# Two-block transformer kernel on one core: products of 512 columns, slots picked head by head, a reordered begin, and a rearranged end of the first attention stage

## The chip, the cores and the metric

The kernel runs on one core of a Trainium2 chip. The time is the device time of one execution in microseconds (us). Of the kernel before there are three runs: median 2908.13 us, from 2906.12 to 2909.43 us. One further execution was profiled, and took 2918.25 us; from its first to its last instruction it spans 2916.5 us, and all rows below come from it.

## The reference

A sequence of 256 tokens with 1024 channels (and a second, `mem`, of 256 tokens) passes through two transformer blocks of two layers each. Cut to what matters here:

```python
# first block, per layer
x = x + g_a * (attention(norm(x) @ w_in) @ w_out)
x = x + g_f * ((silu(h @ w_gate) * (h @ w_up)) @ w_down)     # D_FF = 2816
# second block, per layer
x = x + mixer(...)
x = x + cross_attention(norm(x), norm(mem))                  # xa_wq, xa_wkv, xa_wo
x = x + peer_ffn(norm(x))
# peer_ffn: 8 heads, 128 x 128 experts
scores = q @ sub_keys            # two halves per head
top_s, top_i = top_k(scores, 16)
cand = top_s[0][:, None] + top_s[1][None, :]      # 256 candidates
best_s, best_pos = top_k(cand, 16)
expert_idx = take(top_i[0] * 128 + top_i[1], best_pos)
a = h . u[expert_idx];  y = sum(softmax(best_s) * gelu(a) * v[expert_idx])
```

The kernel computes `a` for all 16384 experts and multiplies by a matrix of gates that is zero outside the picked ones. All large products are in float32 precision by three products of fp32r numbers: a number is split in a high part and a low remainder, and high x high, high x low and low x high are summed.

## The kernel before, in words

**Units.** All weights come as 438 units of 128 x 2048 floats (1 MB), in one order (`lists`). The sync engine (SP) loads a unit into one of three buffers `raw` (`fetch`, L2191). ScalarE (ACT) copies it, rounded, to `whi` (L891, `upto`), VectorE (DVE) subtracts and gets the remainder `wlo` (L1329, `through`), and TensorE (PE) multiplies. `whi` and `wlo` have two buffers each; `whi` of unit k+2 waits until PE has read the high part of unit k. Each engine's program calls `take()` once for each unit, and does its stage work between the calls in written order. There are 48 further loads of modulation weights, which DVE accumulates (`modulate`, L1342, L1345).

**Forms.** In an A unit (`a_unit`) the weight is the stationary operand and the activations move: for each of two groups n of output columns and each q of eight, one product with the high part `hth` (L401) and one with the low part `htl` (L403), each of 256 moving columns, into one half of one PSUM bank; then 16 products of `wlo` with `hth` (L411). That is 48 matmuls of 256 columns. B and C units (`b_unit`, L427 to L438; `c_unit`, L453 to L463) have 24 matmuls of 512 columns, with the activations stationary. The 196 A units that the change touches are: w_gate and w_up of both layers (44), xa_wq (8), peer_wq (16), and the expert matrix u (128). The other 16 keep their form. PE takes banks 4 to 7 in turn where none is named (`Banks.take`), and waits until ACT or DVE has read what the bank held (`clear`).

**The peer stage of a layer.** PE: 8 units pq, each followed by the score products of the head before (L825, banks 0 to 3); then 64 units of u (counted u = 0 to 63); then 64 C units of v. ACT applies GELU to each bank of u (L1277). DVE finds the 16 best by MAX8, FIND_INDEX8 and MATCH_REPLACE8 (`sixteen`, L1777 to L1787; `select_head`), in small steps that `some(us)` hands out between the units: steps of 2.2 nominal us for each pq unit and 2.7 for each u unit below 29. After all eight heads `select_slots` turns positions into expert numbers for one half of the tokens at a time: an IS_EQUAL of 2048 elements (`pick`, L1820), eight multiplications on GpSimd (POOL, L2165), a sum (`red`, L1826). At u = 29 PE transposes the result (L848), and from u = 30 to 57 DVE makes one-hot matrices (`one_hot`, L1897 to L1902), PE multiplies them (`gate`, L838), and DVE applies them (`weigh`, L1912). The other half of the gates is made beside the first 31 C units.

**The feed-forward stage.** For each i of 11: unit g, unit u, then the C unit `down(i - 1)`. ACT applies SiLU to g (L1101), DVE multiplies by u (L1646), ACT and DVE split the result.

**The begin.** The memory's normalized transpose, three units K, the transposes of x, the modulation sums (L375, after eight modulation loads), and the fourth K unit. Then `first_mixer(0)`: 12 B units for q, k, v, the heads' scores, weights and values (`step`), filled up with V units, then two transposes (`out_part`), a `gate_row` (L382), and four C units.

## Time and profile before

| | |
|---|---|
| median of 3 runs | 2908.13 us (2906.12 to 2909.43) |
| profiled execution, its own time | 2918.25 us |
| its span | 2916.5 us |
| TensorE busy | 2818.6 us (97%) |
| VectorE busy | 1971.7 us (68%) |
| ScalarE busy | 1336.6 us (46%) |
| GpSimd busy | 194.7 us (7%) |
| moved by DMA | 537.78 MB, mean 184 GB/s |

Matmuls are pipelined: a row's duration is longer than the distance from one start to the next. The rate of a series is read from the starts.

### The profile page before, as it was taken

To read this page: it belongs to the slowest core of one execution; us is meant where nothing else is said; L and a number is where in the kernel's file an instruction comes from. 1 tells how busy PE (TensorE), PEld (TensorE's weight loads), DVE (VectorE), ACT (ScalarE), POOL (GpSimd) and SP (SyncE) were. 2 spreads that over 40 slices of the span, in tenths; PEclk is the share of its full clock that TensorE was granted. 3 is DMA by queue.
4 is the path that set the end of the run, shared out by engine and by line. 5 is a ranking of instruction groups with operands and counts; after the bars stand their busy time and mean duration, and the time that the engine had idled before them with its cause. 6 is when DMAs were issued, how large, how long until landed. Compare 5 with 4: busy or idle time off the path is not lost.

```text
span 2916.5 us, 45834 instructions
## 1 busy us (share of the span) xinstructions
PE 2818.6 (97%) x19604; PEld 2547.9 (87%) x19604; DVE 1971.7 (68%) x2790; ACT 1336.6 (46%) x1454; POOL 194.7 (7%) x168
## 2 busy tenths in 40 slices
PE   7889999999999899999999999998999999999998
PEld 6768998789988789999988888897899999988887
DVE  6767766664443558877769965535589777699755
ACT  3454435554457444443434444484444534344443
POOL 0200002010003000220000000030000500000000
PEclk9989999999999999999999999999999999999999
DMA  7848864645543345554445555533455544455554
GB/s 294 292 147 303 306 214 148 213 173 188 185 182 130 130 157 176 174 188 160 173 154 193 174 188 193 217 130 118 156 174 177 185 163 170 160 188 174 188 191 148
DMA packets 75658, 537.78 MB, mean 184 GB/s; under 512 B 8512, under 2 KB 8896, under 8 KB 12096
## 3 DMA queue, kind: packets, MB, share of 16 engines
q1 hardware_dynamic: 75456, 534.86, 52.0%
q8 instruction: 155, 2.54, 0.3%
q14 instruction: 47, 0.39, 0.0%
HBM read 527.48 MB, written 7.34 MB: 183 GB/s over the span
## 4 chain that ended last, share of the span: by engine, by line
PE 63%; issue 22%; DVE 6%; POOL 3%; ACT 3%; DMA 2%; SPq 0%; DVEq 0%; POOLq 0%; ACTq 0%
PE bank L401 10%; PE bank L411 10%; PE bank L403 10%; PE bank L453 7%; PE bank L455 6%; PE bank L463 6%; POOL big L2165 2%; PE bank L427 2%; PE bank L429 2%; PE bank L438 2%; DVE wlo L1329 2%; PE bank L491 2%; DMA raw<-in_wkv 1%; PE bank L838 1%; ACT whi L891 1%
## 5 line engine op out<-in xcount | busy, mean ns | idle before, releaser
L891 ACT ACTIVATE whi<-raw 128x2048 fp32r<-128x2048 f32 x438 | 839.3, 1917 | 1073.2 <-PE bank L403 544.8
L1329 DVE TENSOR_TENSOR wlo<-raw,whi 128x2048 fp32r<-128x2048 f32 x438 | 1007.8, 2301 | 424.4 <-ACT whi L891 424.0
L401 PE MATMUL bank<-hth,whi 128*128 128x256 f32 x3392 | 835.1, 286 | 3.4 <-DVE htl L1399 1.9
L403 PE MATMUL bank<-htl,whi 128*128 128x256 f32 x3392 | 824.7, 283 | 0.0
L401 PEld LDWEIGHTS bank<-hth,whi 128*128 128x128 f32 x3392 | 649.4, 191 | 8.7 <-DVE htl L1394 3.3
L403 PEld LDWEIGHTS bank<-htl,whi 128*128 128x128 f32 x3392 | 650.0, 192 | 1.2 <-issue 0.5
L453 PE MATMUL bank<-whi,hth 128*128 128x512 f32 x1152 | 459.1, 399 | 14.4 <-DVE htl L1394 10.0
L455 PE MATMUL bank<-whi,htl 128*128 128x512 f32 x1152 | 451.9, 392 | 0.0
L411 PE MATMUL bank<-hth,wlo 128*128 128x256 f32 x3392 | 441.9, 283 | 1.0 <-DVE wlo L1329 1.0
L411 PEld LDWEIGHTS bank<-hth,wlo 128*128 128x128 f32 x3392 | 422.2, 192 | 1.4 <-DVE wlo L1329 1.4
L463 PE MATMUL bank<-wlo,hth 128*128 128x512 f32 x1152 | 287.4, 389 | 0.0
L453 PEld LDWEIGHTS bank<-whi,hth 128*128 128x128 f32 x1152 | 218.2, 189 | 61.6 <-issue 15.8
L455 PEld LDWEIGHTS bank<-whi,htl 128*128 128x128 f32 x1152 | 218.1, 189 | 44.2 <-issue 0.2
L463 PEld LDWEIGHTS bank<-wlo,hth 128*128 128x128 f32 x1152 | 216.2, 188 | 44.9
L1399 DVE TENSOR_TENSOR htl<-big,hth 128x512 fp32r<-128x512 f32 x144 | 99.3, 690 | 178.7 <-ACT hth L917 178.7
L1912 DVE SCALAR_TENSOR_TENSOR big<-bank,big 128x512 f32<-128x512 f32 x128 | 127.9, 1006 | 25.5 <-PE bank L838 19.6
L427 PE MATMUL bank<-whi,hth 128*128 128x512 f32 x288 | 118.4, 411 | 7.4 <-ACT whi L891 7.4
L429 PE MATMUL bank<-whi,htl 128*128 128x512 f32 x288 | 115.3, 400 | 0.0
L2091 POOL TENSOR_TENSOR small<-small 128x2 f32<-128x2 f32 x12 | 8.4, 702 | 1432.9 <-DVE small L1375 1432.9
L917 ACT ACTIVATE hth<-big 128x512 fp32r<-128x512 f32 x144 | 88.3, 614 | 31.4 <-DVE big L1411 27.8
L2165 POOL TENSOR_TENSOR big<-big 128x256 f32<-128x256 f32 x64 | 77.9, 1256 | 353.7 <-DVE big L1820 353.7
L491 PE MATMUL bank<-small,big 128*128 128x128 f32 x384 | 63.3, 341 | 36.4 <-DVE small L1385 34.0
(255 smaller groups left out, 2978.8 us busy)
## 6 DMA issues: line engine op xcount, KB each, us to landing
raw<-in_pu SPq DMA_DIRECT2D x128, 1024.0 KB, 4.8
raw<-in_pv SPq DMA_DIRECT2D x128, 1024.0 KB, 4.8
raw<-in_win SPq DMA_DIRECT2D x52, 1024.0 KB, 4.8
big<-in_wmod SPq DMA_DIRECT2D x24, 1024.0 KB, 7.2
raw<-in_wmod SPq DMA_DIRECT2D x24, 1024.0 KB, 5.2
raw<-in_wgate SPq DMA_DIRECT2D x22, 1024.0 KB, 4.9
raw<-in_wup SPq DMA_DIRECT2D x22, 1024.0 KB, 5.0
raw<-in_wdown SPq DMA_DIRECT2D x22, 1024.0 KB, 4.9
```

The lines of the kernel that those rows point to most:

```text
L401: e.matmul(o[n], h[:, q, c[n]], H[:, q * 256:(q + 1) * 256], start=n == 0 and q == 0, stop=False, skip_group_check=True)
L403: m = e.matmul(o[n], h[:, q, c[n]], L[:, q * 256:(q + 1) * 256], start=False, stop=False, skip_group_check=True)
L411: m = e.matmul(o[n], w[:, q, c[n]], H[:, q * 256:(q + 1) * 256], start=False, stop=q == 7, skip_group_check=True)
L427: e.matmul(psum(keys[t])[:, :], H[:, o:o + 128], h[:, q, :], start=half == 0 and q == 0, stop=False, skip_group_check=True)
L429: m = e.matmul(psum(keys[t])[:, :], L[:, o:o + 128], h[:, q, :], start=False, stop=False, skip_group_check=True)
L453: e.matmul(bank[i][:, :], H[:, x:x + 128], h[:, q, c], start=opens and q == 0, stop=False, skip_group_check=True)
L455: m = e.matmul(bank[i][:, :], L[:, x:x + 128], h[:, q, c], start=False, stop=False, skip_group_check=True)
L463: m = e.matmul(bank[i][:, :], H[:, x:x + 128], w[:, q, i % 2 * 512:(i % 2 + 1) * 512], start=False, stop=closes and q == 1, skip_group_che ...
L891: e.activation(whi(j), slot[u][0], ACT.Copy).then_inc(*hi.mark(j))
L1329: e.tensor_tensor(wlo(j), slot[u][0], whi(j).bitcast(F32), ALU.subtract).then_inc(*lo.mark(j))
L1912: e.scalar_tensor_tensor(v, product, 1.0 / 1024, v, ALU.mult, ALU.mult).then_inc(*took_v.mark(key))
L2165: e.tensor_tensor(eh, eh, tf, ALU.mult).then_inc(*p_mul.mark((l, "pick", t, w)))
```

## The change

1. `a_unit` becomes `wide_unit` for the 196 units: `hth` and `htl` are interleaved in one tile (`Halves`: for each of 8 chunks 256 columns high, then 256 low), so that one matmul of 512 columns does the work of L401 and L403. It fills a whole bank: the left half gets high x high and (by the 16 matmuls of 256 columns) low x high, the right half high x low. The unit takes two banks, aligned (`Banks.pair`: 4 and 5, or 6 and 7). ACT copies the left halves out (`apart`), DVE adds the right halves (`joined`), and GELU or SiLU is then applied in SBUF, one unit later.
2. The slots are picked head by head (`select_slots(l, h)`, `slots_summed(l, h)`) instead of after all heads; shares and softmax once for all. `some` gets 3.0 for each pq unit from the third, 2.4 for each u below 30. The slots are transposed at u = 32 instead of 29 (`GATES`), and gates are made from u = 32 to 57, two in every fourth unit instead of every eighth.
3. Begin: another order of modulation and K units; x is loaded earlier, lambda and rope gains later; x is transposed before the third K unit, and K units 2 and 3 go to banks 1 and 2.
4. End of the first attention stage of layer 0: the last weights and values use other banks (0, 1, 4 and 6, 7), the first two `out_part` go to step 13, `gate_row(0, 0)` goes behind the second of the four C units, and its modulation loads come earlier.

```diff
+class Halves:
+    def __init__(self, x):
+        v = x.rearrange("p (c h n) -> p c h n", h=2, n=256)
+        self.both, self.hi, self.lo = x, v[:, :, 0], v[:, :, 1]
...
+    def pair(self, key):
+        self.turn += self.turn % 2
+        b = 4 + self.turn % 4
+        self.turn += 2
...
+        def wide_unit(key, M, ready, between=None):
+            for n in range(2):
+                evicted(held[n])
+                for q in range(8):
+                    if n == 0 and q % 2 == 0:
+                        ready(q // 2)
+                    m = e.matmul(bank[b + n], h[:, q, c[n]], M.both[:, q * 512:(q + 1) * 512], start=q == 0, stop=False,
...
+            on.wait_ge(*lo.at(k))
+            for n in range(2):
+                for q in range(8):
+                    m = e.matmul(bank[b + n][:, 0:256], w[:, q, c[n]], M.hi[:, q], start=False, stop=q == 7,
...
-    units += [m0[0], m0[1], k0[0], m0[2], k0[1], m0[3], m0[4], k0[2], *m0[5:], k0[3]]
+    units += [m0[0], m0[1], k0[0], m0[2], m0[3], k0[1], m0[4], m0[5], k0[2], m0[6], m0[7], k0[3]]
...
-            if l == 0:
-                gate_row(0, 0)
             project(("o1", l), ("mix1", l), OO)
...
                 if i == 1:
-                    out_part(name, o, 2)
-                    out_part(name, o, 3)
+                    if stage == ("mix1", 0):
+                        gate_row(0, 0, (4, 5))
+                    for q in (2, 3):
...
+        def apart(dst, key, k):
+            on.wait_ge(*unit.at(k))
+            e.copy(pair(dst), parts(key)[0]).then_inc(*took_a.mark(key))
...
+        def joined(dst, key):
+            on.wait_ge(*took_a.at(key))
+            e.tensor_tensor(pair(dst), parts(key)[1], pair(dst), ALU.add).then_inc(*took_v.mark(key))
...
 # ScalarE, expert units
             for u in range(64):
-                if u in (21, 25):
-                    exponent(u // 25)
+                if u == GATES - 1:
+                    exponent()
                 k = take()
                 upto(k + 2)
-                on.wait_ge(*unit.at(k))
+                if u:
+                    gelu(u - 1)
                 region(on, l, u)
-                e.activation(ag(u * 512, 512), psum(key)[:, :], ACT.Gelu).then_inc(*took_a.mark(key))
+                apart(ag(u * 512, 512), ("a", l, u), k)
+            gelu(63)
...
 # VectorE, expert units
                 take()
+                if u:
+                    activated(u - 1)
+                if u == GATES - 2:
+                    some(1e9)
+                    exponents(l)
+                if u == GATES - 1:
+                    shares(l)
+                if u == GATES:
+                    slots_turned(l, 0)
+                    slots_turned(l, 1)
+                if GATES <= u < 58:
                     gate_step(l, 0, *plan.step(pace(u)))
-                if u < 29:
-                    some(2.7)
+                if u < GATES - 2:
+                    some(2.4)
```

`select_slots(l, h)` does, for both token halves in one instruction each: a cast of 32 indices, shift, mask and two casts of 16, and two IS_EQUAL of 512 elements; POOL multiplies four times 256 elements for each head; `slots_summed` is two sums over 512 elements, done after the next head's search.

## Rows read from the trace of the kernel before

**Rows 1.** The page's first part: busy time, share of the span, instructions
```profile
PE 2818.6 (97%) x19604; PEld 2547.9 (87%) x19604; DVE 1971.7 (68%) x2790; ACT 1336.6 (46%) x1454; POOL 194.7 (7%) x168
```
**Rows 2.** TensorE's waits, expert units of layer 0, 1063 to 1500 us
```profile
PE bank L411 <- DVE wlo L1329: 0.5, 1, 0.5
```
**Rows 3.** Chain of waits, two A units in a row: start us, us, what
```profile
1145.28 1.92 PE bank L411 x16
...
1151.04 1.92 PE bank L411 x16
```
**Rows 4.** Timeline of TensorE, two C units in a row: start us, us, instruction
```profile
1696.90 0.39 PE L453 MATMUL bank<-whi,hth 128*128 128x512 f32 x1
...
1700.53 1.98 PE L463 MATMUL bank<-wlo,hth 128*128 128x512 f32 x8
1702.34 0.39 PE L453 MATMUL bank<-whi,hth 128*128 128x512 f32 x1
```
**Rows 5.** Stretches: start:end us, length, PE, PEld, DVE, ACT, POOL, clock, DMA share, GB/s
```profile
283.17:419.00 135.83, 135.83 (x962) 128.17 (x962) 92.84 (x53) 55.51 (x40) 0.00 (x0) 1.00 0.76 277
1112.00:1170.00 58.00, 58.00 (x486) 58.00 (x486) 54.83 (x193) 27.80 (x23) 0.00 (x0) 1.00 0.55 189
1279.00:1440.00 161.00, 161.00 (x1644) 160.01 (x1643) 119.79 (x168) 63.80 (x52) 0.00 (x0) 1.00 0.50 171
1145.49:1197.31 51.82, 51.82 (x434) 51.82 (x433) 47.45 (x161) 22.19 (x19) 0.00 (x0) 1.00 0.53 183
```
**Rows 6.** Groups of VectorE and ScalarE: shapes, count | busy us, mean ns | idle before
```profile
L1424 DVE TENSOR_TENSOR big<-bank,big 128x512 f32<-128x512 f32 x24 | 16.1, 688 | 10.6 <-PE bank L463 10.6
L1912 DVE SCALAR_TENSOR_TENSOR big<-bank,big 128x512 f32<-128x512 f32 x128 | 127.9, 1006 | 25.5 <-PE bank L838 19.6 <-ACT big L1277 5.9
L1399 DVE TENSOR_TENSOR htl<-big,hth 128x512 fp32r<-128x512 f32 x144 | 99.3, 690 | 178.7 <-ACT hth L917 178.7
L1277 ACT ACTIVATE big<-bank 128x512 f32<-128x512 f32 x128 | 76.4, 597 | 0.6 <-PE bank L411 0.5
```
**Rows 7.** Timeline of VectorE, one unit with gates: start us, us, instruction
```profile
1317.98 2.29 DVE L1329 TENSOR_TENSOR wlo<-raw,whi 128x2048 fp32r<-128x2048 f32 x1 [0.20 <-ACT whi L891]
1320.19 0.42 DVE L1897 TENSOR_TENSOR oh<-iotah,tj 128x512 f16<-128x512 f16 x1
...
1321.80 1.28 DVE L1912 SCALAR_TENSOR_TENSOR big<-bank,big 128x512 f32<-128x512 f32 x2
```
**Rows 8.** Timeline of VectorE while POOL multiplies, 1222 to 1246 us
```profile
1228.35 2.83 DVE L1329 TENSOR_TENSOR wlo<-raw,whi 128x2048 fp32r<-128x2048 f32 x1
1233.21 2.29 DVE L1826 TENSOR_REDUCE big<-big 128x128 f32<-128x2048 f32 x1 [2.03 <-POOL big L2165]
```
**Rows 9.** Groups of GpSimd: the multiplications of the slots
```profile
L2165 POOL TENSOR_TENSOR big<-big 128x256 f32<-128x256 f32 x64 | 77.9, 1256 | 353.7 <-DVE big L1820 353.7
```
**Rows 10.** Timeline of TensorE, first matmul after the last expert unit u
```profile
1501.86 0.76 PE L453 MATMUL bank<-whi,hth 128*128 128x512 f32 x1 [1.98 <-issue]
```
**Rows 11.** The same place as a stretch, columns as in rows 5: eight matmuls
```profile
1501.86:1505.34 3.48, 3.48 (x9) 2.77 (x9) 3.48 (x9) 0.00 (x0) 0.00 (x0) 0.51 0.00 0
```
**Rows 12.** TensorE's waits, begin of the kernel, 0 to 130 us
```profile
PE bank L491 <- DVE small L1385: 11.8, 2, 10.5
PE bank L427 <- ACT whi L891: 6.7, 3, 4.0
PE bank L491 <- ACT big L956: 2.3, 1, 2.3
PE bank L401 <- DVE big L1411: 2.1, 1, 2.1
```
**Rows 13.** TensorE's waits, the last heads of layer 0, 190 to 212 us
```profile
PE bank L574 <- ACT big L1047: 2.6, 1, 2.6
PE bank L562 <- DVE big L1578: 2.2, 2, 1.4
PE bank L544 <- ACT big L950: 1.0, 1, 1.0
```
**Rows 14.** The begin as a stretch, columns as in rows 5
```profile
60.00:115.00 55.00, 49.44 (x218) 40.11 (x216) 42.50 (x58) 23.93 (x26) 14.91 (x3) 0.94 0.76 269
```

More of the change, by code:

```diff
@@ L25 @@
 NRAW = 3
+GATES = 32
 NSP = 2
@@ L91, in take @@
         self.held[b] = key
+        self.where[key] = b
+        return b, before
+    def pair(self, key):
+        self.turn += self.turn % 2
+        b = 4 + self.turn % 4
+        self.turn += 2
+        before = [self.held.get(b), self.held.get(b + 1)]
+        self.held[b] = self.held[b + 1] = key
         self.where[key] = b
@@ L188, in program @@
     IOTAH = at("iotah", 204800 + 4 * 1888, 128, F16)
-    bank = [ctx.enter_context(nc.psum_tensor(f"bank{i}", [P, 512], F32)) for i in range(8)]
+    PS = ctx.enter_context(nc.psum_tensor("banks", [P, 4096], F32))
+    bank = [PS[:, i * 512:(i + 1) * 512] for i in range(8)]
     banks = Banks()
@@ L194, in psum, with parts, pair @@
         return bank[banks.where.get(key, 0)]
+    def parts(key):
+        b = banks.where.get(key, 0)
+        v = PS[:, b * 512:(b + 2) * 512].rearrange("p (n h c) -> p n h c", n=2, h=2)
+        return v[:, :, 0], v[:, :, 1]
+    def pair(x):
+        return x.rearrange("p (c n) -> p c n", n=256)
     def ag(o, n):
@@ L353, in tensor, with evicted @@
         used = [0]
-        def clear(key, b=None):
-            b, held = banks.take(key, b)
+        def evicted(held):
             if took_a.has(held):
@@ L360, in clear @@
                 on.wait_ge(*took_v.at(held))
+        def clear(key, b=None):
+            b, held = banks.take(key, b)
+            evicted(held)
             return b
@@ L389, in take, with a_unit @@
             return k
-        def a_unit(key, H, L, ready, between=None, b=None):
+        def wide_unit(key, M, ready, between=None):
+            k = take()
+            b, held = banks.pair(key)
+            h, w = whi(k).rearrange("p (k n) -> p k n", k=8), wlo(k).rearrange("p (k n) -> p k n", k=8)
+            c = [slice(n * 128, (n + 1) * 128) for n in range(2)]
+            for n in range(2):
[4 more added lines that the diff above has]
+                    m = e.matmul(bank[b + n], h[:, q, c[n]], M.both[:, q * 512:(q + 1) * 512], start=q == 0, stop=False,
+                                 skip_group_check=True)
+                if n == 0 and between is not None:
+                    between()
+            m.then_inc(*hi_read.mark(k))
+            on.wait_ge(*lo.at(k))
+            for n in range(2):
+                for q in range(8):
+                    m = e.matmul(bank[b + n][:, 0:256], w[:, q, c[n]], M.hi[:, q], start=False, stop=q == 7,
+                                 skip_group_check=True)
+            m.then_inc(*unit.mark(k))
+            return k
+        def a_unit(key, M, ready, between=None, b=None):
             k = take()
@@ L531, in first_mixer @@
                     turn_query(nb - 3)
-                b_unit(keys, HTH, HTL, 1, lambda q: normed(on, name, q))
+                b_unit(keys, HT, 1, lambda q: normed(on, name, q))
             turn_query(3)
             def scores(nq, hs):
-                of = [bank[clear(("s", l, nq, h))] for h in hs]
+                last = l == 0 and nq and hs[0] == 6
+                of = [bank[clear(("s", l, nq, h), 4 + h % 2 if last else None)] for h in hs]
                 on.wait_ge(*took_a.at(("qt", l, nq, 1)))
@@ L583, in step @@
                     scores(2, (2 * (i - 8), 2 * (i - 8) + 1))
+                if l == 0 and i == 13:
+                    for q in range(2):
+                        out_part(("o1", l), OO, q, 5 - 5 * q)
                 if 2 <= i < 14:
@@ L1094, in feed_forward @@
             for i in range(11):
+                gate, hd = (ag(PR + 1024 * x + (i % 2) * 512, 512) for x in range(2))
                 k = take()
                 upto(k + 2)
-                on.wait_ge(*unit.at(k))
                 if i >= 2:
@@ L1198, in query @@
                 key = ("xq", l, h)
-                on.wait_ge(*unit.at(k))
                 since()
-                e.copy(ag(QTX + h * 512, 512), psum(key)[:, :]).then_inc(*took_a.mark(key))
+                apart(ag(QTX + h * 512, 512), key, k)
                 last_h[0] = k
@@ L1258, in peer @@
                     k = take()
[L1259 to L1260 removed]
                     since()
[L1262 removed]
+                    apart(ag(QT + i * 512, 512), ("pq", l, i), k)
                 if i:
@@ L1633, in feed_forward @@
             for i in range(11):
+                gate, hd = (ag(PR + 1024 * x + (i % 2) * 512, 512) for x in range(2))
                 k = take()
@@ L1865, in selection, with slots_summed @@
+        def slots_summed(l, h):
+            for w in range(2):
+                on.wait_ge(*p_mul.at((l, "pick", h, w)))
+                dst = ag(II, 768).rearrange("p (t w k) -> p t w k", t=2, w=3)[:, :, w, h * 16:(h + 1) * 16]
+                e.tensor_reduce(dst, picked(h, w), X, ALU.add).then_inc(*top.mark((l, "red", h, w)))
+                yield 0.65
         def selection(l):
```

387 lines of the change are left out of this document (198 added, 189 removed).

## The prediction

> **What bounds the kernel now.** I read the page's busy times first: TensorE is busy in 97% of the span, VectorE in 68% [rows 1]. Then TensorE's waits by stage. From 1063 to 1500 us, the pq and u units of a layer, it waits 0.5 us in all [rows 2]; nothing is to be had there but fewer or cheaper matmuls. The begin and the last heads of layer 0 are where it does wait [rows 12, 13]. Third, the rate. Sixteen matmuls of 256 columns take 1.92 us, 120 ns each, and an A unit repeats every 5.76 us, which is 48 of them [rows 3]. A C unit repeats every 5.44 us, 24 matmuls of 512 columns at 226.7 ns, and its first 16 take 3.63 us [rows 4]. At 2.4 GHz the columns alone are 106.7 and 213.3 ns, so about 13.3 ns per matmul come on top at either length. That is what fewer, longer matmuls can save. Last, VectorE by stage: 54.8 of 58 us busy at u = 0 to 9, 119.8 of 161 in the stage with gates, 92.8 of 135.8 in the feed-forward [rows 5]. The engine that gets new work is nearly full exactly where most of the changed units are.
>
> **The change, part by part.**
>
> *Wide matmuls.* Per unit 32 matmuls of 256 columns (3.84 us) become 16 of 512 (3.63 us at the rate of rows 4); the 16 low ones stay. A unit goes from 5.76 to 5.55 us, 0.214 less; times 196 units, -42 us. All lies on the path, since TensorE sets it. Bounds: no saving, if a 512 costs two 256 (0), and 16 x (240 - 213.3) = 0.43 us per unit (-84), if the extra vanished. I take the C unit's rate: the same length, a new stationary block for each matmul as here.
>
> The trace shows 120 ns where columns take 106.7 [rows 3]. The Trainium skill (TensorE: Matmul & The Clock Gate, "Back-to-back issue gap") gives a warm gap of columns / 2.4 + 2.5 ns; by it a pair is worth 2.5 ns and this part an estimated 8 us, not 42. The trace does not agree with the 2.5.
>
> *New eviction.* ACT now copies the left halves (0.60 us, the nearest row is GELU out of a bank) and applies GELU or SiLU later from SBUF (0.6 again) [rows 6]. Its load is 27.8 of 58 us [rows 5], so +0.6 per unit is covered by TensorE's 5.55. DVE adds the right halves. Nearest row: one bank and one SBUF input of 512, 688 ns; upper bound the strided 1006 ns [rows 6]. I take 0.66 to 0.69, the plain add. In the feed-forward, DVE has 92.8 of 135.8 us, eight triples; two adds per triple make 104 of 132: covered, as is ACT. The `down` unit needs its input only two units later. Cross attention: the pairs make q2 and q3 wait for the add of the unit before, about 1.4 us after it, behind score products of about that length: nothing.
>
> *DVE while slots are picked, u = 0 to 29.* From 1145.49 to 1197.31 us lie nine units and three heads; DVE is busy 47.45 us [rows 5]. Less nine `wlo` at 2.21 (distance of starts, rows 7) that is 9.2 us per head. New per head are two IS_EQUAL and two sums over 512 elements at about 0.66 (as L1399, rows 6) and five tiny ones, 0.65 together: 3.3. So 12.5 us per head for a nominal 11.7; a handful of 2.4 nominal costs 2.56. DVE per unit: 2.21 + 0.67 + 2.56 = 5.44, beside TensorE's 5.55. POOL's 64 multiplications of 1.26 us [rows 9] no longer come in a block behind the search but 5 us in each head. While POOL runs, `wlo` takes 2.83 instead of 2.29 us, while a sum with one input keeps its 2.29 [rows 8]. One `wlo` and one IS_EQUAL per head meet it: +0.7 per head, +0.14 per unit: 5.58. A tie. Handfuls are uneven, and a late add holds up TensorE's next pair: I take 2 us per layer, +4. Bounds: 0 (5.44 is below 5.55) and, with an add of 1.0 us, 5.9, that is 0.35 x 30 x 2 = +21.
>
> That only two-input operations stretch fits the Trainium skill (SBUF — State Buffer, "Who interferes with whom"): such a DVE instruction and a GpSimd one that reads SBUF contend, and the loser fully blocks. By full blocking each such meeting could cost a whole POOL instruction; that is in the third rival.
>
> *Gates in 26 instead of 28 units.* DVE per unit: 2.21 + 0.67 + one-hot 1.61 (1320.19 to 1321.80) + 0.65 for applying [rows 7], 5.1; with two gates 7.4. TensorE needs 6.1 to 6.65. Sum over 26 units: about 147 against 157 to 162 us. Covered, 0.
>
> *The transposes at u = 32.* They take two banks, which are unit 30's; unit 32's aligned pair is then unit 31's, just finished. It waits for `joined(31)`, which on DVE stands behind `wlo` of the unit after next: 2.2 + 0.7 = 2.9 us, less 0.6 for the transposes. A stall of 2.4 us in each layer. After the idle 1.98 us at 1501.86 [rows 10] the granted clock was 0.51, the lower of its two levels (1.2 GHz), and eight 512s took 3.48 instead of 1.81 us [rows 11]: +1.7. So +4.1 per layer, +8. Bounds: 2.4 and 4.1 per layer.
>
> *From u to v.* That 1.98 us is GELU, split, remainder. Now it is copy 0.6, add 0.7, GELU 0.6, split 0.6, remainder 0.7: 3.3, +1.3 per layer, +2.6. The slow clock there is already paid. *The last score of pq* waits for an add more, 0.6 per layer, +1.2.
>
> *Begin.* The K units, 5.8 us each, now partly stand between the transposes and the modulation sums. The waits for the diagonal behind a modulation load, the 2.3 and 2.1 us [rows 12] can shrink, and the first B unit can start some 4 us earlier. But then come waits for `whi`, 6.7 us, behind DMA at 269 GB/s and 76% [rows 12, 14], which take back part. Lambda and rope gains are issued behind the first freed raw buffer, at about 25 us, and are needed at 47 and 67 us. I take -3; bounds 0 and -12 (half of the 22.9 us in rows 12). *End of the stage:* the waits of the last heads, 5.8 us [rows 13], get 1 us of transposes to fill them, and the gate row fills another gap: -2; bounds 0 and -4.
>
> **Sum:** -42 + 4 + 8 + 2.6 + 1.2 - 3 - 2 = -31 us. The profiled execution, 2918.25 us of its own, would take 2887; its time is 10.1 us above the median shown, and the difference goes against the median: **2908.1 - 31 = 2877 us**. Of this, TensorE's matmuls are -42 and the new waits +16.
>
> **The rivals.**
>
> (1) *DVE is a little over TensorE while slots are picked.* Add at 1.0 us, 5.9 per unit, +21 instead of +4: 2894 us. For: DVE had 54.8 of 58 us. Against: the plain add from a bank is 0.69. Chance 0.18.
>
> (2) *The begin gives more.* If the reordering gives back some 20 us of the idle in rows 12 and 13, 2862 us. For: 28.7 us stand there. Against: DMA at 269 GB/s. Chance 0.10.
>
> (3) *Slower: DVE becomes the bound of the expert units.* Without DVE's term the sum is -35, so it decides from a loss of 35 us in the 60 units below u = 30: 5.55 + 0.58 = 6.1 us of DVE per unit. Adds at 1.0 (+0.33) and three DVE operations per head blocked by a whole POOL instruction of 1.26 us (3.8 / 4.9 units = +0.77) give 5.44 + 1.1 = 6.5: +57, so 2930 us. For: two-input operations do stretch [rows 8]. Against: by 0.54, not by 1.26. Chance 0.05.
>
> (4) *The change doesn't save what it says:* if only a fifth of the 13.3 ns per pair were saved in this form (weights stationary, activations moving), the first part gives 8 us and the whole is +3: 2911 us. This is the time to which the page's 2.5 ns leads. Against: C units show the full amount [rows 4]. Chance 0.03.
>
> **How the numbers follow.** Forecast 0.64, with a range of its own of 2864 to 2890. About 0.2% (6 us) can be told from no change. Forecast, (1) and (2) are faster by more: 0.92. (4) is within: 0.03. (3) is slower: 0.05. Range 2858 to 2898: it takes in (1) and (2) at their values and leaves out (3), (4) and the far ends of (1) and (2).
>
> **What would show it.** Right: A units of u repeat every 5.55 us, with 16 matmuls of 512 in 3.63; `joined` takes 0.69; before unit 32 TensorE idles about 2.4 us in each layer, with a clock below 1.00 behind it, and before v = 0 about 3.3 us; DVE is over 95% busy for u below 30. Wrong: a period of 5.7 or more with waits for DVE (rival 1 or 3); `wlo` often at 2.8 us or more; pairs of starts 240 ns apart (rival 4); TensorE waiting in the feed-forward, which I cost at nothing; or a begin shorter by more than 10 us (rival 2).

## The result, and the profile after

The changed kernel takes 2902.1 us (median of 16 runs, 2898.9 to 2906.4). The kernel before, with as many runs in turn on the same chips, takes 2916.4 us (2906.1 to 2926.4). The ratio is 0.9953, 95% interval 0.9942 to 0.9965: about 14 us faster. The forecast was 2877 us, 31 us below the median shown then. Some 8 us of the miss in the absolute time come from that base: 2908.1 us was the median of three runs, and the wider sample lies at 2916.4, close to the profiled execution's 2918.25. The other 17 us are the change's own: it gained half of what the sum said.

The page of the kernel after, first its busy times, then the groups that are new (line, engine, operation, names and shapes, count | busy us, mean ns | idle before):

```profile
PE 2791.4 (96%) x16468; PEld 2382.6 (82%) x16468; DVE 2090.9 (72%) x3086; ACT 1408.0 (49%) x1620; POOL 192.0 (7%) x168
...
L428 PE MATMUL banks<-ht,whi 128*128 128x512 f32 x3136 | 771.5, 395 | 7.4 <-DVE big L1470 5.4
...
L976 ACT COPY big<-banks 128x512 f32<-128x512 f32 x196 | 112.2, 572 | 72.7 <-PE banks L436 72.2
L1470 DVE TENSOR_TENSOR big<-banks,big 128x512 f32<-128x512 f32 x196 | 133.8, 683 | 9.7 <-ACT big L976 9.0
```

Against [rows 1], 3136 matmuls are gone (196 units times 16). The new add, `joined` (L1470), takes 683 ns: the plain add of [rows 6], as taken. The new copy takes 572 ns.

The timeline of TensorE, one wide expert unit and the start of the next (start us, us, instruction), answers to [rows 3]:

```profile
1130.48 3.82 PE L428 MATMUL banks<-ht,whi 128*128 128x512 f32 x16
1134.13 2.08 PE L436 MATMUL banks<-ht,wlo 128*128 128x256 f32 x16
1136.04 1.32 PE L428 MATMUL banks<-ht,whi 128*128 128x512 f32 x5
```

Sixteen wide products take 3.65 us from start to start, 228 ns each, and the unit repeats every 5.56 us where it took 5.76. That is close to the forecast for a unit that holds nothing else (3.63 and 5.55 us). TensorE's waits of the expert stage of layer 0, 1063 to 1500 us, tell more. [Rows 2] had 0.5 us of waits for the low parts, and the 1.98 us of [rows 10] behind the last unit:

```profile
PE banks L503 <- DVE ht L1465: 3.9, 1, 3.9
...
PE banks L880 <- DVE big L1470: 3.0, 1, 3.0
PE banks L428 <- DVE big L1470: 2.7, 1, 2.7
```

Three single waits, all behind the new chain of copy and add. Stretches of the kernel after (columns as in [rows 5]): the feed-forward; early expert units in two pieces, slots being picked; just behind the wait at unit 32; units with gates.

```profile
283.17:419.00 135.83, 135.83 (x728) 117.73 (x727) 102.59 (x70) 65.70 (x59) 0.00 (x0) 1.00 0.77 279
...
1106.30:1161.90 55.60, 55.60 (x321) 49.18 (x320) 55.15 (x141) 30.06 (x30) 12.60 (x10) 1.00 0.55 189
1161.90:1278.80 116.90, 116.90 (x673) 103.30 (x673) 109.38 (x281) 62.75 (x65) 22.49 (x19) 1.00 0.55 190
1284.30:1288.00 3.70, 3.69 (x9) 2.93 (x10) 3.67 (x11) 0.00 (x0) 0.00 (x0) 0.54 0.87 283
1304.50:1480.00 175.50, 175.50 (x1376) 151.86 (x1375) 145.66 (x199) 82.50 (x87) 0.00 (x0) 1.00 0.50 169
```

In the first ten units in which slots are picked, VectorE is busy 55.15 of 55.60 us, 99%, in the next 21 units 109.38 of 116.90, 94%, and TensorE does not wait once. The tie that the forecast saw is there in the first ten, and it costs nothing.

Everything below is measured with one ruler, worked out from TensorE's timeline of one execution of each kernel: the distance from the first product of the first query unit of an expert stage to the first product of its first down unit, in parts. Here and in all runs, us, layer 0 / layer 1 where they differ:

| kernel | queries to u=0 | u=0 to 31 | 31 to 32 | 32 to 63 | 63 to v=0 | sum |
|---|---|---|---|---|---|---|
| before | 53.89 | 180.07 | 6.31 | 195.19 | 7.89 | 443.4 |
| after | 56.60 / 56.42 | 172.66 / 174.16 | 9.10 | 192.35 | 9.58 | 440.3 / 441.6 |
| E1 slots' banks | 56.56 / 56.42 | 172.66 / 174.15 | 6.14 | 191.66 | 9.58 | 436.6 / 438.0 |
| E2 add first | 53.71 / 53.75 | 175.42 / 175.44 | 9.10 | 190.76 | 9.58 | 438.6 |
| E3 narrow ends | 53.08 / 53.50 | 174.45 / 174.41 | 9.10 | 192.3 | 8.39 | 437.3 / 437.8 |
| E4 = E1 and E3 | 53.06 | 174.44 | 6.14 | 191.66 | 8.39 | 433.7 |
| E5 two of 256 | 57.03 / 57.15 | 180.13 / 179.67 | 9.29 | 195.56 / 197.04 | 9.76 | 451.8 / 452.9 |
| E6 slots part alone | 53.89 | 178.64 | 6.33 | 195.57 | 7.90 | 442.3 |
| E7 more picking | 56.46 / 56.58 | 181.27 / 181.30 | 9.10 | 192.34 | 9.58 | 448.8 / 448.9 |
| E8 four pairs | 53.06 / 53.48 | 172.67 | 6.18 | 191.68 | 8.40 | 432.0 / 432.4 |
| E10 E8, GELU first | 53.44 | 172.67 | 6.18 | 191.69 | 7.94 | 431.9 |

One thing disturbs this ruler. After a wait of 2.6 to 3 us TensorE's granted clock is sometimes 1.00 and sometimes near the lower of its two levels, and the lower level makes the unit behind the wait 1.0 to 1.6 us longer. This is in unit 0 (second part) or unit 32 (fourth part), and it is named below where a comparison hangs on it.

An expert stage gave only 3.1 and 1.7 us up to the down units, 2.4 on average. In the profiled execution (span 2916.5 before, 2900.3 after) the rest of the 16.2 us comes from the two feed-forwards, 4.3 and 3.5, and from the begin and first attention stage, 4.6 (237.3 to 232.8 us); the other stages together take about 1 us more than before.

### The profile page after: what moved, and what is told of

Its sections match the earlier page's. It is cut to its first block and busy times, and to the rows that moved or that the text cites. A ratio compares the mean times of both kernels' runs of the same rounds, so it can differ in the third digit from the quotient of the medians.

```text
span 2900.3 us, 40006 instructions
## 1 busy us (share of the span) xinstructions
PE 2791.4 (96%) x16468; PEld 2382.6 (82%) x16468; DVE 2090.9 (72%) x3086; ACT 1408.0 (49%) x1620; POOL 192.0 (7%) x168
## 5 line engine op out<-in xcount | busy, mean ns | idle before, releaser
L428 PE MATMUL banks<-ht,whi 128*128 128x512 f32 x3136 | 771.5, 395 | 7.4 <-DVE big L1470 5.4
L428 PEld LDWEIGHTS banks<-ht,whi 128*128 128x128 f32 x3136 | 576.5, 189 | 123.3 <-issue 6.9
L503 PE MATMUL banks<-whi,ht 128*128 128x512 f32 x1152 | 459.6, 399 | 18.2 <-DVE ht L1460 10.0
L505 PE MATMUL banks<-whi,ht 128*128 128x512 f32 x1152 | 452.7, 393 | 0.0
L436 PEld LDWEIGHTS banks<-ht,wlo 128*128 128x128 f32 x3136 | 401.9, 191 | 15.8
L436 PE MATMUL banks<-ht,wlo 128*128 128x256 f32 x3136 | 406.6, 283 | 0.0
L513 PE MATMUL banks<-wlo,ht 128*128 128x512 f32 x1152 | 287.4, 389 | 0.0
L503 PEld LDWEIGHTS banks<-whi,ht 128*128 128x128 f32 x1152 | 218.6, 190 | 65.3 <-issue 19.3
L505 PEld LDWEIGHTS banks<-whi,ht 128*128 128x128 f32 x1152 | 218.7, 190 | 44.3
L513 PEld LDWEIGHTS banks<-wlo,ht 128*128 128x128 f32 x1152 | 216.2, 188 | 44.9
L1470 DVE TENSOR_TENSOR big<-banks,big 128x512 f32<-128x512 f32 x196 | 133.8, 683 | 9.7 <-ACT big L976 9.0
L2002 DVE SCALAR_TENSOR_TENSOR big<-banks,big 128x512 f32<-128x512 f32 x128 | 127.3, 1005 | 18.4 <-PE banks L893 18.4
L477 PE MATMUL banks<-whi,ht 128*128 128x512 f32 x288 | 116.9, 406 | 8.2 <-ACT whi L946 8.2
L479 PE MATMUL banks<-whi,ht 128*128 128x512 f32 x288 | 114.0, 396 | 0.0
```

The source lines that it names most:

```text
L428: m = e.matmul(bank[b + n], h[:, q, c[n]], M.both[:, q * 512:(q + 1) * 512], start=q == 0, stop=False, skip_group_check=True)
L436: m = e.matmul(bank[b + n][:, 0:256], w[:, q, c[n]], M.hi[:, q], start=False, stop=q == 7, skip_group_check=True)
L477: e.matmul(psum(keys[t])[:, :], M.hi[:, half * 4 + q, o], h[:, q, :], start=half == 0 and q == 0, stop=False, skip_group_check=True)
L479: m = e.matmul(psum(keys[t])[:, :], M.lo[:, half * 4 + q, o], h[:, q, :], start=False, stop=False, skip_group_check=True)
L503: e.matmul(bank[i][:, :], M.hi[:, o + q, x], h[:, q, c], start=opens and q == 0, stop=False, skip_group_check=True)
L505: m = e.matmul(bank[i][:, :], M.lo[:, o + q, x], h[:, q, c], start=False, stop=False, skip_group_check=True)
```

## The experiments

Each run is compared, as the change was, with runs of the kernel before on the same chip; a difference from the kernel after is that of the two ratios times 2917 us, and is uncertain by some 5 us. The table above is the sharper measure.

**E1. The slots' transposes in other banks.**

```diff
-                        b = clear(("top", l, t))
+                        b = clear(("top", l, t), 2 + t)
```

> The changed kernel, but the transposes of the picked slots at unit 32 go to banks 2 and 3 (used by the scores long before) instead of banks 4 and 5, so that unit 32 takes the pair of banks that unit 30 used and not the one that unit 31 has just filled. Theory A (time is lost where PE waits for the sum of a pair of banks): the 2.7 us wait of PE for the sum of unit 31 goes, and with it the stretch of slow clock behind it; unit 32 takes 6.2 to 6.5 us from the start of the transposes where it took 10.8, so about -4.5 us per layer, -9 us in all, ratio to the kernel before 0.9953 to about 0.992. Rival B (VectorE has no room here and is late anyway, so that the wait moves to the next units): the units 33 to 36 take up the time, and the total changes by less than 2 us.

Measured: 2895.8 us, ratio 0.9919 (0.9905 to 0.9933), 10 us less than after; 3.7 us per layer in the table, 7.3 in all. The place before, in the kernel after, and then in E1 (timeline of TensorE):

```profile
1280.79 0.85 PE L903 MATMUL banks<-small,big 128*128 128x128 f32 x6
1284.31 5.50 PE L428 MATMUL banks<-ht,whi 128*128 128x512 f32 x16 [2.68 <-DVE big L1470]
1289.65 2.07 PE L436 MATMUL banks<-ht,wlo 128*128 128x256 f32 x16
```

```profile
1281.50 0.82 PE L903 MATMUL banks<-small,big 128*128 128x128 f32 x6
1282.07 3.91 PE L428 MATMUL banks<-ht,whi 128*128 128x512 f32 x16
1285.82 2.08 PE L436 MATMUL banks<-ht,wlo 128*128 128x256 f32 x16
...
1289.57 0.64 PE L893 MATMUL banks<-oh 128*128 128x64 f16 x16
1290.94 0.64 PE L893 MATMUL banks<-oh 128*128 128x64 f16 x16 [0.73 <-DVE oh L1992]
```

The wait and the slow products behind it (granted clock 0.54 in 1284.30 to 1288.00) are gone; from the start of the transposes to unit 33 it is 6.23 us instead of 10.77. Of these 4.5 us 0.9 come back in unit 33 (7.53 us in E1, 6.63 after), at a gate whose one-hots VectorE has not ready: another wait was hidden behind this one. Theory A holds, at four fifths of its size.

**E2. VectorE makes the last query sum first.**

```diff
-                    some(3.0 if i > 1 else 0.0)
+                    some({1: 0.0, 7: 0.0, 8: 6.0}.get(i, 3.0))
```

> The changed kernel, but VectorE picks nothing between the sums of query units 6 and 7 of an expert stage, and twice as much right behind the sum of unit 7. No operation is added or removed. Theory A: the last score of the queries waits for a sum that VectorE could have made 3 us sooner; PE's wait of 3.0 us falls to about 0.5 us, the interval of that score from 10.7 and 12.4 us to about 8, so -3 to -4 us per layer, about -7 us in all, ratio about 0.993. Rival B (the cost is VectorE's load, not its order): the double handful makes the weights' low parts of the first units late, PE waits there, and the total changes by less than 2 us.

Measured: 2901.3 us, ratio 0.9938 (0.9924 to 0.9951), 4 us less than after. The cause is seen in the timeline of VectorE in the kernel after:

```profile
1096.75 0.68 DVE L1470 TENSOR_TENSOR big<-banks,big 128x512 f32<-128x512 f32 x1
1097.35 0.75 DVE L1878 TENSOR_TENSOR big<-big 128x256 f32<-128x256 f32 x2
...
1100.25 0.74 DVE L1865 MAX8 big<-big 128x8 f32<-128x256 f32 x2
1100.91 0.67 DVE L1470 TENSOR_TENSOR big<-banks,big 128x512 f32<-128x512 f32 x1
```

Between the sums of query units 6 and 7 stands a whole handful of picking, 3.6 us, while TensorE stands still for 2.99 us before the last score at 1101.64. In E2 (timeline of TensorE) that wait is 0.41 us, and a new one of 2.56 us stands before unit 2:

```profile
1102.09 1.16 PE L880 MATMUL banks<-big 128*128 128x128 f32 x8 [0.41 <-DVE big L1470]
...
1116.94 3.42 PE L428 MATMUL banks<-ht,whi 128*128 128x512 f32 x14 [2.56 <-DVE big L1470]
```

So both theories name something real. The order on VectorE made the wait; but the work moved behind the sum made VectorE late, and unit 2, which takes unit 0's pair of banks, paid for it. The table shows 2.9 and 2.7 us won up to u=0 and, in layer 0, 2.8 lost behind it. (In layer 1 the kernel after had lost 1.5 us there, in a stretch of slow clock behind the wait; that went, and the net loss is 1.3.) Unit 32 met no slow clock in this run, though TensorE's wait before it was as long as ever, 2.67 us. That is worth 1.6 us per layer in the fourth part and is not the edit's doing by any path that I can name. Without it the edit gains 1.5 us in both layers together, 1.4 of them in layer 1 by the slow clock that went, and that is less than the 2 us that theory B allowed: in the total it is B that holds.

**E3. Query unit 7 and unit 63 narrow again.** ScalarE takes the whole result out of one bank, and VectorE adds nothing there.

```diff
-                    wide_unit(("pq", l, i), HT, ready)
+                    (wide_unit if i < 7 else a_unit)(("pq", l, i), HT, ready)
...
-                wide_unit(("a", l, u), HT, ready, between)
+                (wide_unit if u < 63 else a_unit)(("a", l, u), HT, ready, between)
...
-                apart(ag(u * 512, 512), ("a", l, u), k)
-            gelu(63)
+                if u < 63:
+                    apart(ag(u * 512, 512), ("a", l, u), k)
+            on.wait_ge(*unit.at(k))
+            e.activation(ag(63 * 512, 512), psum(("a", l, 63))[:, :], ACT.Gelu).then_inc(*took_a.mark(("a", l, 63)))
...
```

> The changed kernel, but the two units of an expert stage whose result PE needs at once (query unit 7 and unit 63) are again made with 32 products of 256 columns into one bank, copied (or passed through GELU) by ScalarE alone, with no sum on VectorE. Theory A (the wait belongs to the chain copy, sum, GELU behind a wide unit): each of the four units costs 0.2 to 0.45 us more on PE, the last score falls from 10.7 and 12.4 us to about 7.8, and the gap between unit 63 and the first down unit from 3.85 to about 2.0 us (11.0 to 9.4 us with the products around it); about -5 us per layer, -10 us in all, ratio about 0.992. Rival B (VectorE's load or the slow clock at the change of stage makes these waits, whatever the form of the last unit): under 2 us.

Measured: 2889.2 us, ratio 0.9895 (0.9878 to 0.9911). The table gives 3.0 and 3.9 us per layer, 6.9 in all; the ratio says 17, with some 6 us of uncertainty, and I go by the table, though its execution was the longest of E3's four (2900.7 us; the others took 2886.8 to 2890.5). Why the whole time gained more than the expert stages is open. The last score no longer waits (queries to u=0: 53.1 to 53.5 us, below the kernel before). Waits of TensorE in E3, 1040 to 1500 us:

```profile
PE banks L428 <- DVE big L1476: 4.2, 2, 2.7
...
PE banks L503 <- DVE ht L1471: 2.5, 1, 2.5
```

The 4.2 us are unit 32's 2.7 and 1.5 us at unit 2: VectorE is still behind there, with the handful that now follows query unit 7. The gap behind unit 63 fell by 1.2 us, less than the 1.7 that the change had added.

**E4. E1 and E3 together.**

> Narrow query unit 7 and unit 63 together with the slots' transposes in banks 2 and 3. Theory A: the places lie apart on the path, so the two savings add up, -9 and -10 us to about -19 us, 2883 us, ratio about 0.989. Rival B (one VectorE schedule behind all of them): less than the larger one of the two alone plus 2 us.

Measured: 2890.3 us, ratio 0.9895 (0.988 to 0.9911). In the table 433.7 us per layer, 6.6 and 7.9 below the kernel after; E1 gave 3.7 and E3 3.0 and 3.9, so the sum would be 6.7 and 7.5. They add up, as theory A has it; in the whole time, 17 us by the ratios, E4 is not told apart from E3.

**E5. The wide product taken apart.** All units, sums and orders as in the kernel after, but two products of 256 columns for each of 512.

```diff
-                    m = e.matmul(bank[b + n], h[:, q, c[n]], M.both[:, q * 512:(q + 1) * 512], start=q == 0, stop=False,
-                                 skip_group_check=True)
+                    e.matmul(bank[b + n][:, 0:256], h[:, q, c[n]], M.hi[:, q], start=q == 0, stop=False,
+                             skip_group_check=True)
+                    m = e.matmul(bank[b + n][:, 256:512], h[:, q, c[n]], M.lo[:, q], start=False, stop=False,
+                                 skip_group_check=True)
```

> The changed kernel with all its two-bank units, sums and schedule, but each product of 512 columns is made as two of 256 again (the tile's high part into the first half of the bank, its low part into the second). This prices the wide product alone. Theory A (the unit's period is set by PE): the high part of a unit goes from 3.65 to about 3.84 us, the period from 5.565 to about 5.76, 196 units, +38 us, ratio about 1.008; the waits for the sums get shorter by what PE is later, so a little less, +30 to +38. Rival B (the units run at VectorE's pace, so PE's gain was already eaten): under +15 us.

Measured: 2935.2 us, ratio 1.0059 (1.0044 to 1.0074), so the wide form is worth 31 us; theory A holds, at the low end of its 30 to 38. Stage by stage it is 11.5 and 11.3 us for the two expert stages, 4.3 and 3.7 us for the two feed-forwards (200.1 against 195.8, 204.3 against 200.6 us), 30.8 in these four. A unit with nothing else in it gains 0.195 us, close to the 0.214 of the forecast. One with gates gains three quarters of it, 0.15 us: with one gate it takes 6.31 us in E5 and 6.16 in the kernel after, with two 6.77 and 6.63. The fourth part of the table says this in layer 1 alone, where it is 197.04 against 192.35, 0.15 per unit. In layer 0 it is 195.56 against 192.35, but there unit 32 met full clock in E5 (5.83 us) and the lower level in the kernel after (7.25 us). Unit 0 of layer 0 was the other way round (7.33 us in E5, 5.66 after), so that the sum of the layer is right by luck. Unit 32 of E5, its first 3.7 us in layer 0 and in layer 1 (columns as in [rows 5]):

```profile
1302.36:1306.06 3.70, 3.69 (x31) 3.70 (x32) 3.67 (x11) 0.00 (x0) 0.00 (x0) 1.00 0.83 283
2347.95:2351.65 3.70, 3.70 (x21) 3.70 (x22) 3.67 (x11) 0.00 (x0) 0.00 (x0) 0.65 0.79 288
```

The timelines of TensorE show where a unit with one gate loses part of the gain. First E5, then the kernel after:

```profile
1314.97 0.28 PE L428 MATMUL banks<-ht,whi 128*128 128x256 f32 x1
...
1316.89 0.64 PE L895 MATMUL banks<-oh 128*128 128x64 f16 x16
...
1319.36 2.08 PE L438 MATMUL banks<-ht,wlo 128*128 128x256 f32 x16
```

```profile
1304.35 2.00 PE L428 MATMUL banks<-ht,whi 128*128 128x512 f32 x8
1306.19 0.64 PE L893 MATMUL banks<-oh 128*128 128x64 f16 x16
1306.67 2.09 PE L428 MATMUL banks<-ht,whi 128*128 128x512 f32 x8
1308.60 2.07 PE L436 MATMUL banks<-ht,wlo 128*128 128x256 f32 x16
```

Eight wide products take 1.84 us ahead of the gate, where E5's sixteen take 1.92, and 1.93 behind it; in E5 gate and second half together take 2.47 us (1316.89 to 1319.36), here 2.41. The first half gains 0.08 and the second 0.06 us: the products right behind a gate take 0.09 us more than those ahead of it, and a quarter of the unit's gain is lost there. Of the two rules weighed in the forecast the trace's own 13.3 ns per product held (16 pairs give 0.195 us, 12 ns a pair). By the Trainium skill (TensorE: Matmul & The Clock Gate, "Back-to-back issue gap") a pair is worth an estimated 2.5 ns, 8 us in all, and these runs do not agree with it.

**E6. The slots part alone, on the kernel before.** The slots picked head by head, multiplied on GpSimd between, turned at unit 32, denser gates; products of 256 and no sums, and handfuls of 2.2 and 2.7 nominal us as before.

```diff
+GATES = 32
...
-                if u == 29:
+                if u == GATES:
...
-            for t in range(2):
-                yield from select_slots(l, t)
+                if h:
+                    yield from slots_summed(l, h - 1)
+                yield from select_slots(l, h)
...
```

> The kernel before with the slots part of the change alone: each head's slots picked right behind the head on VectorE and multiplied on GpSimd, the turned slots at unit 32 in place of 29, the first half's gates from unit 32. Products stay 256 columns wide into one bank, with no sums. Theory A (this part lies beside PE): no wait of PE for a sum exists here, so the ratio is 0.998 to 1.002. Rival B (the small loss per unit that gates show in the changed kernel comes from the denser gates of this part): +2 to +4 us, ratio 1.001 to 1.0015, with gated units about 0.05 us longer than before.

Measured: 2915.2 us, ratio 0.9988 (0.9976 to 0.9999): most likely 3.5 us faster, within theory A's bounds ("beside PE"). The table says why there is anything: units 0 to 31 take 1.43 us less, the transposes that stood at unit 29 and a wait for a low part in unit 26 (6.51 us, here 5.76), and units 32 to 63 take 0.38 more, because all the gates now stand there. In sum it is 1.0 us per layer. A unit with one gate takes 6.31 us here as in the kernel before, so rival B, a longer gated unit, is out. My forecast had no term for the stop at unit 29 that goes.

**E7. More picking beside each unit.** `some(2.4)` becomes `some(3.0)`; the same operations, sooner.

> The changed kernel with VectorE picking 3.0 us worth of the planner's costs beside each early expert unit in place of 2.4, so it is finished some five units sooner; no operation is added. VectorE is busy 55.15 of 55.60 us there already. Theory A (PE has no slack left to give VectorE: a unit's period is the larger of the two engines' work, one unit of lag is covered by the two pairs of banks): the period rises from 5.565 to about 5.9 to 6.1 us for some 22 units and PE waits for sums and low parts in each, +6 to +11 us per layer, ratio about 1.0 to 1.004. Rival B (VectorE catches up within the lag the banks allow): under +3 us in all.

Measured: 2919.2 us, ratio 1.0006 (0.9996 to 1.0016): 15.5 us more than after, all of it in units 0 to 31 (8.6 and 7.1 us per layer). A stretch (columns as before), and then the timeline of TensorE in E7 at its first wait:

```profile
1106.30:1161.90 55.60, 54.38 (x315) 47.95 (x314) 55.60 (x171) 30.17 (x30) 12.80 (x11) 1.00 0.53 178
```

```profile
1145.63 2.07 PE L436 MATMUL banks<-ht,wlo 128*128 128x256 f32 x16
1148.91 1.39 PE L428 MATMUL banks<-ht,whi 128*128 128x512 f32 x5 [1.22 <-DVE big L1470]
```

For eight units VectorE falls behind and nothing is seen. Then, from unit 8 on, TensorE waits for the sum of the unit two before it, 4.7 us in six waits of layer 0; 1.5 us of layer 0's 8.6 are slow clock at unit 0, as layer 1 of the kernel after has it, and the rest are tenths in the units around the waits. Theory A holds. VectorE at 99% costs nothing, and 0.6 nominal us more per unit cost 7.1 us in either layer, slow clock apart: the kernel after stands at this edge. The rivals (1) and (3) of the forecast name a real mechanism, which the measured 0.68 us of the add keeps out.

**E8. Four pairs of banks.** E3, and units 0 to 31 in turn in four pairs instead of two, the slots' transposes in banks 0 and 1.

```diff
-                wide_unit(("a", l, u), HT, ready, between)
+                if u < 32:
+                    wide_unit(("a", l, u), HT, ready, between, (4, 6, 0, 2)[u % 4])
...
-                        b = clear(("top", l, t))
+                        b = clear(("top", l, t), t)
...
```

> The kernel with narrow query unit 7 and unit 63, and units 0 to 31 in four pairs of banks in turn in place of two (the slots' transposes in banks 0 and 1), so that a unit waits for the sum of the unit four before it. Theory A (what PE waits for at unit 2 and unit 32 is the pair of banks, and VectorE's lag beyond one unit is otherwise harmless): both waits go; per layer the stretch from the first turn of the stage's input to the first down unit falls from 446.9 us (changed kernel) to about 437.5 us, that is 1.5 us below the narrow-ends kernel with the transposes moved (439.0), about 2880 us in all, ratio 0.989 to 0.987. Rival B (VectorE's lag would then hit the weights' low parts instead): PE waits for the low parts, and no gain beyond 439.0 us.

Measured: 2882.4 us, ratio 0.9879 (0.986 to 0.9898). Units 0 to 31 take 172.67 us, exactly 31 periods of 5.57; the wait at unit 2 that E3 and E4 had is gone. Waits of TensorE, 1045 to 1500 us, all there is:

```profile
PE banks L504 <- DVE ht L1477: 2.5, 1, 2.5
PE banks L894 <- DVE oh L2004: 0.8, 1, 0.8
```

Theory A: what TensorE waited for was the pair of banks. (The expectation's "stretch" counts from the turn of the stage's input: 437.4 us were expected, 437.4 and 438.9 measured, against 446.7 and 447.1 in the kernel after; the table's 432.0 and 432.4 leave out the turn, which itself differs by 1.1 us from layer to layer.)

**E9. The begin in the old order.** The order of the first weights and modulation blocks, of the tokens' turn and of the first transfers as before, and the K units' banks in turn as before; the rest as after.

```diff
-    units += [m0[0], m0[1], k0[0], m0[2], m0[3], k0[1], m0[4], m0[5], k0[2], m0[6], m0[7], k0[3]]
+    units += [m0[0], m0[1], k0[0], m0[2], k0[1], m0[3], m0[4], k0[2], *m0[5:], k0[3]]
...
```

> The changed kernel with the begin of the program in the order of the kernel before: the first memory-key weights and the modulation blocks in the old order, the tokens' turn behind the third key unit, the old order of the first transfers. The end of the first attention stage stays as changed. Theory A (the begin is worth what its rows showed, the third query unit starting at 72.7 in place of 77.0 us): +4 to +6 us, ratio 0.9953 to 0.997, with the third query unit at about 77 us again. Rival B (the first 240 us differ between executions of one kernel by as much, and the next wait for weights eats the gain): within 1.5 us, ratio below 0.996, although the third query unit starts later.

Measured: 2907.6 us, ratio 0.9969 (0.9957 to 0.998), 4.6 us more than after; and the expert stages as in the kernel after to 0.05 us. The third query unit in E9, and then in the kernel after (timeline of TensorE):

```profile
75.86 0.56 PE L477 MATMUL banks<-whi,ht 128*128 128x512 f32 x1 [3.16 <-ACT whi L945]
```

```profile
72.66 0.79 PE L477 MATMUL banks<-whi,ht 128*128 128x512 f32 x1 [6.16 <-ACT whi L946]
```

The new begin brings the query units forward by 6 to 7 us and then waits 3 us longer for weights, as the forecast said; 3.2 us are left here. By the ratios 4.6 us are left at the end, with an uncertainty of 5 us, so that the whole time alone would not exclude a value near nothing. At the modulation sums that end the first attention stage the two profiled executions are 7 us apart (239.7 and 232.7 us), which is within what executions of one begin differ by (last section). The 3.2 us and the ratio speak for theory A; the size is known to a few us only.

**E10. GELU of unit 62 first.** In E8, beside unit 63, ScalarE makes the GELU of unit 62 ahead of the next high part.

```diff
+                if u == 63:
+                    gelu(62)
                 upto(k + 2)
-                if u:
+                if 0 < u < 63:
                     gelu(u - 1)
```

> The four-pairs kernel, and beside unit 63 ScalarE makes the GELU of unit 62 ahead of the next weights' high part in place of behind it, so that it is done before unit 63 ends. Theory A (the 0.5 us by which the gap behind unit 63 is still longer than in the kernel before is that GELU): the stretch from unit 63's start to the first down unit falls from 8.40 to about 7.9 us, -1 us in all, ratio 0.987 to 0.988. Rival B (the high part of the next weights becomes what is late): 8.4 us or more, no gain.

Measured: 2883.2 us, ratio 0.9885 (0.9871 to 0.99). The wait before the first down unit is 2.0 us where E8 had 2.5, and 63 to v=0 is 7.94, as in the kernel before: theory A in the part, and nothing that the whole time could show. How the chain stood in the kernel after (timeline, ScalarE, VectorE and TensorE behind unit 63):

```profile
1482.38 0.61 ACT L1335 ACTIVATE big<-big 128x512 f32<-128x512 f32 x1
1482.90 0.57 ACT L976 COPY big<-banks 128x512 f32<-128x512 f32 x1
1483.50 0.69 DVE L1470 TENSOR_TENSOR big<-banks,big 128x512 f32<-128x512 f32 x1 [3.67 <-ACT big L976]
1484.22 0.63 ACT L1335 ACTIVATE big<-big 128x512 f32<-128x512 f32 x1 [0.76 <-DVE big L1470]
1484.76 1.13 ACT L972 ACTIVATE ht<-big 128x512 fp32r<-128x512 f32 x2
1485.41 0.69 DVE L1465 TENSOR_TENSOR ht<-big,ht 128x512 fp32r<-128x512 f32 x1 [1.21 <-ACT ht L972]
...
1486.24 0.77 PE L503 MATMUL banks<-whi,ht 128*128 128x512 f32 x1 [3.85 <-DVE ht L1465]
```

The first of these is the GELU of unit 62, which stood in the way of unit 63's copy. E8 and E10 are the fastest versions, 34 to 35 us below the kernel before by their ratios, where the change as made is 14 below.

## Why the prediction was wrong

The sum beside what was measured, both layers together, us. All are rows of one execution of each kernel; for the first, E5's ratio gives the same.

| step | forecast | measured | from |
|---|---|---|---|
| wide matmuls | -42 | -31 | E5 |
| VectorE while slots are picked | +4 | 0 | no wait for u = 1 to 31 |
| stall at unit 32 | +8 | +9.1 | 2 x (2.96 + 1.59), units 31 and 32 of after and E1 |
| last score of the queries | +1.2 | +7.9 | 3.1 and 3.3, and 1.5 of slow clock |
| from u to v | +2.6 | +3.7 | 2 x (1.69 + the 0.19 that the wide unit 63 saves) |
| begin and end of first stage | -5 | -4.6 | 237.3 to 232.8, uncertain by some us; E9 for the begin |
| slots part: stop at unit 29 gone, gates moved | 0 | -2.0 | 2 x 1.0; E6 |
| all other stages | 0 | +1 | spans |
| sum | -31 | -15.9 | span: -16.2 |

The sum closes to 0.3 us. Two terms made the miss, with 11 and 7 us; VectorE's term, 4 us too high, took some of it back.

**The term of the wide matmuls (-42) was too large.** The step was "0.214 less; times 196 units". The rate was nearly right for a unit that holds nothing else: 0.195 us, and the 44 feed-forward units, the 64 early expert units and the 12 last ones have it or come close. But 52 expert units, u=32 to 57, have small products in their middle, and 16 belong to the queries, with the scores' products between. E5 shows 0.15 us for the first kind; for the second, the seven intervals from query unit 0 to 7 take 46.31 and 45.92 us in E5 and 45.87 and 45.58 in the kernel after, 0.05 to 0.06 per unit. By these rows, as an estimate, the queries make 2.6 of the 11 us, the units with gates 3.5, and the rate itself (0.195 for 0.214 in the other 120) 2.3; the rest lies in the eight units of cross attention (21.83 us in E5 and 21.50 after for three intervals of layer 0) and in what one execution of each can't settle. I had looked at two C units in a row for the rate and never at a product that follows one of another shape, although the trace before had them in every one of those units.

**The last score (+1.2) was too small by 6.7 us.** "Waits for an add more, 0.6 per layer" priced the operation, and not the queue in front of it. The change adds a wait, and the rule that I followed at unit 32 (what stands ahead of the add on VectorE?) was not applied here: a handful of picking of 3.6 us. That the wait also drew a stretch of slow clock behind it, in layer 1 only (5.41 us for the next sixteen products instead of 3.9), was not foreseen either. E2 and E3 both take the wait away, in two ways, and both pay at unit 2 (2.7 and 1.7 us) for VectorE's backlog; with E8's four pairs of banks nothing is paid there.

**What was right.** The pair of banks at unit 32: forecast 2.4 us idle and 1.7 of clock, measured 2.68 and 1.6, and E1 recovers most of it. The clock's part was no certainty, though: behind the same wait E2 in both layers, and E5 in layer 0, kept the full clock, so that here the forecast was also lucky. The begin: the mechanism with its second wait for weights (E9), and the size as far as it can be read. From u to v: 1.3 against 1.9 us, and most of the rest is the GELU of unit 62 (E10 wins 0.45). The feed-forward, the cross attention and ScalarE at nothing: the feed-forward gave its 4.3 us in one layer and 3.5 in the other, VectorE with 102.6 of 135.8 us there. The gates: VectorE with 145.7 of 175.5 us, below TensorE; TensorE's own loss there is in the first term.

**VectorE's +4 and the rivals.** The estimate of 5.44 to 5.58 us per unit fits the first ten units (55.15 us, 5.5 each); over the next 21 it is 5.2 (109.38 us). The error was to price a tie: with one unit of lag allowed by the two pairs of banks, uneven handfuls do not add up as long as the mean is below TensorE's. E7 shows what is beyond. GpSimd's multiplications did not bring the blocking of a whole operation that rival (3) needed: the 438 low parts take 2.30 us in the mean after, beside 2.29 for one undisturbed in [rows 7], and the longest takes 2.87. One IS_EQUAL beside a multiplication took 1.23 us instead of 0.69 (1107.58 us), again half a microsecond more. The Trainium skill (SBUF — State Buffer, "Who interferes with whom") would allow such a block; no run here shows one. Rival (4), that the wide form saves a fifth, is refuted by E5; rival (2) by 4.6 us at the begin.

The range failed at its upper end, 2898, which came from one rival alone, VectorE. The bounds of the small terms ("0.6", and the full rate for mixed units) were not in it, and neither was the base: three runs of before said 2908 where sixteen say 2916.

## What to carry to other kernels

Where a change puts a second engine into an eviction, price each consumer that needs the result at once by what stands ahead of the new operation in that engine's queue, and keep the old form for just those units: four narrow units and a rotation of four pairs of banks (E8) more than doubled the gain. A saving per instruction measured in a run of equal instructions has to be measured again in units that mix shapes: here three quarters of it were left with gates in the unit, and less than a third in the query units. And here an engine at 99% beside the bound cost nothing until its backlog exceeded what the buffers allow: count buffers, and not percentages. Last, compare two kernels unit by unit, and not by the sum of a stage alone: a stretch of slow clock that one of them met by chance is as large as the effect of eight to ten units.

## What the runs showed that was not expected

Eight wide products right behind small ones of another shape cost some 0.09 us more than their like (1.93 against 1.84 us). The same 2.99 us wait before the last query score was followed by full clock in layer 0 (1.00 over the next 3.70 us) and by the lower level in layer 1:

```profile
2137.99:2141.69 3.70, 3.70 (x12) 2.93 (x12) 2.92 (x9) 2.40 (x2) 1.42 (x2) 0.57 0.00 0
1102.55:1106.25 3.70, 3.70 (x19) 3.08 (x18) 3.12 (x9) 2.40 (x2) 1.48 (x2) 1.00 0.00 0
```

E9, with the same code in the expert stages, shows the same pair: 172.65 and 174.14 us. At unit 32 the clock behind the wait of 2.67 us was 1.00 in E2 and 0.54 in the kernel after (2.68 us). What decides between them is open. And while the expert stages repeat to within 0.05 us from run to run, the modulation sums at the end of the first stage, in nine executions that share the begin of the kernel after, started between 229.5 and 237.9 us: a change there of a few us can't be read from one profile of each kernel.
